# Six of eight depth chunks of each expert's gate and up product as three fp32r products, the rest parts of two of them by GpSimd

## The reference

```python
def expert_block(args):
    xb, gb = args
    h = jax.nn.silu(jnp.einsum('td,edf->tef', xb, w_gate)) * jnp.einsum('td,edf->tef', xb, w_up)
    return jnp.einsum('tef,efd->td', h * gb[:, :, None], w_down)
```

## Time and profile before

| | |
|---|---|
| times of three runs | 1206.55, 1212.63, 1216.0 us |
| the profiled execution: span from its first to its last instruction | 1206.0 us (the page gives no other time of it) |
| TensorE busy, matmuls | 1135.6 us, 94% |
| VectorE | 931.7 us, 77% |
| ScalarE | 482.0 us, 40% |
| GpSimd | 228.7 us, 19% |
| chain of waits | TensorE 88%, VectorE 5%, DMA 4%, ScalarE 2% |
| in the chain, by line | L758 18%, L785 15%, L763 14% |
| moved by DMA | 335.68 MB |

### The profile page before, as it was taken

One profiled execution on the slowest core, in us unless ns is written; L12 is line 12 of the kernel. 1 busy time (PEld: TensorE's weight loads), 2 busy tenths in 40 slices (PEclk: granted clock), 3 DMA queues, 4 the chain that ended last, 5 costly groups with the idle time before them and its releaser, 6 DMA issues.

```text
span 1206.0 us, 14783 instructions
## 1 busy us (share of the span) xinstructions
PE 1135.6 (94%) x4802; PEld 761.9 (63%) x4802; DVE 931.7 (77%) x1381; ACT 482.0 (40%) x622; POOL 228.7 (19%) x119
## 2 busy tenths in 40 slices
PE   2799999987999999999999999999999999999986
PEld 2453446875654477677777777777777777777632
DVE  4578997976533777998888888888888888888856
ACT  0214323345650022344444444444444444444411
POOL 0000000000000000122222222222222222223660
PEclk9799999998999989999999999999999999999998
DMA  9993421209202063799999999999999999999892
GB/s 349 369 397 85 50 27 70 71 19 347 89 16 90 35 267 117 299 366 388 382 385 380 384 386 379 373 386 373 397 382 381 377 375 385 373 379 398 319 374 114
DMA packets 77817, 335.68 MB, mean 278 GB/s; under 512 B 14376, under 2 KB 16296, under 8 KB 52824
## 3 DMA queue, kind: packets, MB, share of 16 engines
q1 hardware_dynamic: 58680, 293.15, 64.6%
q0 software_dynamic: 13824, 33.58, 7.6%
q10 hardware_dynamic: 5280, 8.53, 2.1%
HBM read 309.51 MB, written 42.48 MB: 292 GB/s over the span
## 4 chain that ended last, share of the span: by engine, by line
PE 88%; DVE 5%; DMA 4%; ACT 2%; issue 1%; ACTq 0%; SPq 0%; DVEq 0%; POOLq 0%
PE ps L758 18%; PE ps L785 15%; PE ps L763 14%; PE ps L1528 8%; PE ps L813 5%; PE ps L1758 5%; PE ps L1536 3%; PE ps L823 2%; PE ps L1599 2%; DMA ring<-in_w_ada 2%; PE ps L1622 2%; PE ps L1612 2%; PE ps L1728 2%; PE ps L880 1%; PE ps L1556 1%; PE ps L771 1%
## 5 line engine op out<-in xcount | busy, mean ns | idle before, releaser
L567 POOL DMA_INDIRECT xg<-u_rows,idx x64 | 182.7, 2855 | 489.2 <-DVE idx L1056 488.9
L758 PE MATMUL ps<-wx,xT 128*128 128x512 f32 x512 | 235.4, 602 | 0.0
L927 DVE TENSOR_TENSOR gu_lo<-wx,gu_hi 128x2048 fp32r<-128x2048 f32 x64 | 146.6, 2291 | 57.0 <-ACT gu_hi L646 57.0
L922 DVE TENSOR_TENSOR wd_lo<-wx,wd_hi 128x2048 fp32r<-128x2048 f32 x65 | 148.5, 2285 | 2.8 <-ACT wd_hi L1486 2.2
L758 PEld LDWEIGHTS ps<-wx,xT 128*128 128x128 f32 x512 | 92.1, 190 | 91.9 <-issue 91.8
L659 ACT ACTIVATE hs<-ps 128x256 f32<-128x256 f32 x68 | 26.1, 383 | 302.3 <-PE ps L763 281.7
L639 ACT ACTIVATE wd_hi<-wx 128x2048 fp32r<-128x2048 f32 x64 | 122.5, 1913 | 26.6 <-PE ps L785 26.6
L763 PE MATMUL ps<-gu_hi,xT_hi 128*128 128x512 f32 x256 | 126.2, 493 | 0.4 <-DVE gu_lo L927 0.4
L646 ACT ACTIVATE gu_hi<-wx 128x2048 fp32r<-128x2048 f32 x64 | 122.1, 1908 | 0.0
L785 PE MATMUL ps<-wd_hi,hT_hi 128*128 128x512 f32 x272 | 111.8, 411 | 2.9 <-DVE hT_lo L941 2.9
L785 PE MATMUL ps<-wd_hi,hT_lo 128*128 128x512 f32 x272 | 107.3, 395 | 0.0
(11 more groups left out here) (317 smaller groups left out, 1873.8 us busy)
## 6 DMA issues: line engine op xcount, KB each, us to landing
wx<-in_w_gate SPq DMA_DIRECT2D x64, 1024.0 KB, 7.8
wx<-in_w_up SPq DMA_DIRECT2D x64, 1024.0 KB, 10.9
wx<-in_w_down SPq DMA_DIRECT2D x64, 1024.0 KB, 8.5
expert_rows<-yrow SPq DMA_DIRECT2D x64, 512.0 KB
ring<-in_w_ada SPq DMA_DIRECT2D x7, 2048.0 KB, 19.1
ring<-in_w_in SPq DMA_DIRECT2D x6, 2048.0 KB, 15.9
vg<-in_w_ada SPq DMA_DIRECT2D x2, 2048.0 KB, 13.1
fk<-in_w_ada SPq DMA_DIRECT2D x2, 2048.0 KB, 14.9
```

The source lines that it names most:

```text
L567: pool.indirect_dma_start(out=xg[:, buf, :], out_offset=None, in_=u2_d[:, :], in_offset=bass.IndirectOffsetOnAxis(ap=idx[:, col:col + 1], ...
L758: pe.matmul(bank, xT_raw[:, j - J3, :], raw[:, :, j, :], start=(j == J3), stop=False)
L922: dve.tensor_tensor(wd_lo[s][:], w, wd_hi[:].bitcast(F32), ALU.subtract).then_inc(wd_ready, 1)
L927: dve.tensor_tensor(gu_lo[s][:, :, 0:J3, :], gate_up_weights(s)[:, :, 0:J3, :], gu_hi[:].bitcast(F32), ALU.subtract).then_inc(gu_lo_ready, 1)
```

## The change

J3, the number of split chunks, goes from 4 to 6; JA = 4 is the first group. TensorE multiplies two chunks in full, then the twelve products of chunks 0 to 3, then six products of chunks 4 and 5. The weights' high parts of chunks 4 and 5 get a buffer and a ScalarE instruction of their own (gu_hi2, gate_up_high2); their rest parts are made by GpSimd (gate_up_low2) into the same gu_lo. A new semaphore, gu_half, tells when the first twelve products are done; gate_up_high waits for that and stands ahead of silu. The turned rows' parts are made in two pieces, chunks 4 and 5 (from ps3) first. hT_hi moves into space shared with another tile.

```diff
-J3 = 4
+JA, J3 = 4, 6
...
+            def gate_up_low2(s, n):
+                pool.wait_ge(gu_hi2_ready, n + 1)
+                pool.tensor_tensor(gu_lo[s][:, :, JA:J3, :], gate_up_weights(s)[:, :, JA:J3, :], gu_hi2[:].bitcast(F32),
+                                   ALU.subtract).then_inc(gu_lo2_ready, 1)
...
-            def expert(i, u):
+            def expert(i, u, ending=False):
 
-                pool.wait_ge(idx_ready, i + (u + 3))
-                pool.reg_add(last, zero, T - 1)
-                gather((u + 2) % 4, u % 2, last)
+                if not ending or u < UNROLL - 2:
+                    pool.wait_ge(idx_ready, i + (u + 3))
+                    pool.reg_add(last, zero, T - 1)
+                    gather((u + 2) % 4, u % 2, last)
+                if not ending or u < UNROLL - 1:
+                    gate_up_low2((u + 1) % UNROLL, i + (u + 1))
...
             pairs(0, 7)
-            expert(tail, 1)
+            expert(tail, 1, True)
             pool.wait_ge(gu_done, n_steps + (VIRT - 2))
             pairs(1, 7)
             pool.wait_ge(y_stored, 16 * n_steps)
             pairs(0, 5)
             pairs(1, 5)
+            expert(tail, 2, True)
...
                 if used is not None:
+                    act.wait_ge(gu_half, used - VIRT)
+                act.activation(gu_hi[:], gate_up_weights(s)[:, :, 0:JA, :], ACT.Copy).then_inc(gu_hi_ready, 1)
+
+            def gate_up_high2(s, used):
+                if used is not None:
                     act.wait_ge(gu_done, used)
-                act.activation(gu_hi[:], gate_up_weights(s)[:, :, 0:J3, :], ACT.Copy).then_inc(gu_hi_ready, 1)
+                act.activation(gu_hi2[:], gate_up_weights(s)[:, :, JA:J3, :], ACT.Copy).then_inc(gu_hi2_ready, 1)
 
             def rows_high(n):
                 act.wait_ge(xt2_done, n + 1)
-                act.activation(xT_hi[:], ps[2][:, 0:J3 * P].rearrange("p (j n) -> p j n", n=P), ACT.Copy).then_inc(xt2_act, 1)
+                act.activation(xT_hi[:, JA:J3, :], ps[3][:, 0:(J3 - JA) * P].rearrange("p (j n) -> p j n", n=P),
+                               ACT.Copy).then_inc(xt2_act, 1)
+                act.activation(xT_hi[:, 0:JA, :], ps[2][:].rearrange("p (j n) -> p j n", n=P), ACT.Copy).then_inc(xt2_act, 1)
...
+                if more:
+                    gate_up_high((u + 1) % UNROLL, 8 * i + (32 if u < UNROLL - 1 else 64), i + (VIRT + u + 1))
                 silu_gate(i + (VIRT + u), u)
                 if more:
                     rows_high(i + (u + 1))
                     if first and u == 0:
                         shared_out(3)
-                    gate_up_high((u + 1) % UNROLL, 8 * i + (32 if u < UNROLL - 1 else 64), i + (VIRT + u + 1))
+                    gate_up_high2((u + 1) % UNROLL, i + (VIRT + u + 1))
...
-                pe.wait_ge(xt2_dve, n - VIRT + 1)
+                pe.wait_ge(xt2_dve, 2 * n - 2 * VIRT + 2)
                 pe.wait_ge(gu_lo_ready, n - VIRT + 1)
-                for j in range(J3):
-                    for k, (a, w) in enumerate(((xT_hi, gu_hi), (xT_hi, gu_lo[u]), (xT_lo, gu_hi))):
-                        mm = pe.matmul(bank, a[:, j, :], w[:, :, j, :], start=False, stop=(j == J3 - 1 and k == 2))
+                for j in range(JA):
+                    for a, w in ((xT_hi, gu_hi), (xT_hi, gu_lo[u]), (xT_lo, gu_hi)):
+                        mm = pe.matmul(bank, a[:, j, :], w[:, :, j, :], start=False, stop=False)
+                mm.then_inc(gu_half, 1)
+                pe.wait_ge(gu_lo2_ready, n - VIRT + 1)
+                for j in range(JA, J3):
+                    rest = gu_lo[u][:, :, j, :]
+                    for k, (a, w) in enumerate(((xT_hi, gu_hi2[:, :, j - JA, :]), (xT_hi, rest), (xT_lo, gu_hi2[:, :, j - JA, :]))):
+                        mm = pe.matmul(bank, a[:, j, :], w, start=False, stop=(j == J3 - 1 and k == 2))
                 mm.then_inc(gu_done, 1)
...
             def rows_low(n):
-                dve.wait_ge(xt2_done, n + 1)
-                dve.tensor_copy(xT_raw, ps[3][:, 0:(KD - J3) * P].rearrange("p (j n) -> p j n", n=P)).then_inc(xt_raw_ready, 1)
+                dve.wait_ge(xt2_act, 2 * n + 1)
+                dve.tensor_copy(xT_raw, ps[3][:, (J3 - JA) * P:].rearrange("p (j n) -> p j n", n=P)).then_inc(xt_raw_ready, 1)
                 dve.wait_ge(xt_raw_ready, n + 1)
-                dve.wait_ge(xt2_act, n + 1)
-                dve.tensor_tensor(xT_lo[:], ps[2][:, 0:J3 * P].rearrange("p (j n) -> p j n", n=P), xT_hi[:].bitcast(F32),
-                                  ALU.subtract).then_inc(xt2_dve, 1)
+                dve.tensor_tensor(xT_lo[:, JA:J3, :], ps[3][:, 0:(J3 - JA) * P].rearrange("p (j n) -> p j n", n=P),
+                                  xT_hi[:, JA:J3, :].bitcast(F32), ALU.subtract).then_inc(xt2_dve, 1)
+                dve.wait_ge(xt2_act, 2 * n + 2)
+                dve.tensor_tensor(xT_lo[:, 0:JA, :], ps[2][:].rearrange("p (j n) -> p j n", n=P),
+                                  xT_hi[:, 0:JA, :].bitcast(F32), ALU.subtract).then_inc(xt2_dve, 1)
```

More of the change, by code:

```diff
@@ L107, in build @@
             hT_lo = sb("hT_lo", [P, 2, KF, P], F32R, at=over)
+            hT_hi = sb("hT_hi", [P, 2, KF, P], F32R, at=over)
         vg = sb("vg", [P, NT, 2, 512])
         with ExitStack() as over:
-            gu_hi = sb("gu_hi", [P, 2, J3, ED], F32R, at=over)
+            gu_hi = sb("gu_hi", [P, 2, JA, ED], F32R, at=over)
         with ExitStack() as over:
@@ L202, in build @@
         hs = sb("hs", [P, 2, ED])
-        hT_hi = sb("hT_hi", [P, 2, KF, P], F32R)
         sel1 = sb("sel1", [P, 2, NT, P], BF16)
@@ L409, in build @@
         gu_lo_ready = sem("gu_lo_ready")
+        gu_hi2_ready = sem("gu_hi2_ready")
+        gu_lo2_ready = sem("gu_lo2_ready")
+        gu_half = sem("gu_half")
         y_stored = sem("y_stored")
@@ L420, in build @@
         out_stored = sem("out_stored")
+        gu_hi2 = sb("gu_hi2", [P, 2, J3 - JA, ED], F32R)
         tri8 = sb("tri8", [P, 64])
@@ L574, in pool_tail @@
                 gather(k, k)
+            gate_up_low2(0, 0)
             n_steps = steps(pool)
@@ L591, in pool_tail @@
             tail = pool.snap(pool.to_reg(n_steps - UNROLL), min_val=NE - UNROLL, max_val=MAXPASS * NE)
-            expert(tail, 0)
+            expert(tail, 0, True)
             def rows_of(t, k):
@@ L682, in act_tail @@
             gate_up_high(0, 32, None)
+            gate_up_high2(0, None)
             silu_gate(2, 2)
@@ L882, in gated @@
                 mm.then_inc(yg_summed, 1)
-            pe.wait_ge(xt2_act, n_steps)
-            pe.wait_ge(xt2_dve, n_steps)
+            pe.wait_ge(xt2_act, 2 * n_steps)
+            pe.wait_ge(xt2_dve, 2 * n_steps)
             pe.wait_ge(idx_ready, n_steps)
```

2 lines of the change are left out of this document (1 added, 1 removed).

## The result

The changed kernel took 1221.16 us (median of 4 runs, 1214.94 to 1234.65) beside 1210.07 for the kernel before: a ratio of 1.007 (95% interval 1.0038 to 1.0103; it leaves the run at 1234.65 out as disturbed). It is slower by a little, where I forecast 1210 and no measurable change. The profiled runs have spans of 1213.0 and 1206.0 us, 7.0 apart.

The account below looks back on a forecast made before the run. TensorE alone was taken as the bound, 10.27 us per expert. 57 x 0.33 = 18.8 us saved, 16 lost: -2.8 us, hence 1210 us, no measurable change; its own range 1200 to 1222, with rivals 1193 to 1335.

Parts of the forecast that it names:

- TensorE's saving: Per expert, 4 full records less and 6 split products more: 0.33 us less, a period of 9.94 us.
- Who goes first in the loop: Both subtracts ready near T+2.9, T being the next rows' first turn; VectorE's gu_lo first by 0.02 to 0.06 us.
- the other side: Rival: GpSimd's subtract goes first in every expert, TensorE starts 1.86 us late each time, 1315 us; chance 0.27.
- GpSimd's subtract: Rest parts of chunks 4 and 5: 2.2 us of work, row about 4.5 us with its wait for gu_lo.
- The step that failed: Experts with a 1.21 us VectorE instruction before gu_lo: GpSimd gets in first, 2.7 us net lost, five times, 13.6 us.
- forecast -2.8: Whole span: 18.8 us saved in 57 experts less 16 us lost elsewhere, on a span of 1206.0 us.
- The expert of rows 9: First expert, which already waits for gu_lo in the kernel before: gets some 2 us later.
- The tail: Behind the loop, two GpSimd subtracts stand between row fetches: 0 to 2 us.
- so gu_lo goes first and the loss is 0.4: Last expert of the tail: GpSimd still issues fetches until 1133.8, so VectorE's gu_lo precedes its subtract; loss 0.4 us.
- Rival 4 (the memory): Loop's weight loads fall 0.23 us behind per expert; some 4 us lost, with no room 1223 us; chance 0.07.

Follow-up runs that it names:

- experiment 2: Changed kernel with GpSimd's subtract replaced by a plain write of zeros, rest parts of chunks four and five left out: 1196.89 us, ratio 0.9883.
- experiment 4: Changed kernel with three extra TensorE products filling the stall in five experts: 1226.88 us, ratio 1.012; an earlier version with six products took 1232.26.
- experiment 5: Changed kernel with two row fetches at the end moved ahead of GpSimd's subtract of the last expert but one: 1231.86 us, inconclusive as a time.
- experiment 9: The changed kernel run again with no edit: 1214.97, 1216.84, 1230.91 and 1233.55 us, ratio 1.0146.
- e18: Changed kernel with each row fetch of the loop bringing half a row, the other half left out: 1215.46 us, ratio 1.0046.
- e1: Changed kernel with one added wait, GpSimd's subtract starting only when VectorE's gu_lo is done: 1207.23 us, ratio 0.9972.
- e7: Changed kernel; GpSimd's subtract waits for gu_lo, two end fetches go before the subtract, one_hots stands behind hT_lo: 1205.35 us, ratio 0.9942.
- e9: e7 without its moved end fetches, and with VectorE making the rest parts of the last three experts: 1198.73 us, ratio 0.9904.
- e10: e9 with the shared expert's operations moved out of the first and last experts to behind the loop: 1188.54 us, ratio 0.9835.

## Why the prediction was wrong

- **TensorE's saving: right.** 9.93 us against a forecast of 9.94, in 55 periods.
- **Who goes first in the loop, and for how long: right.** I had the margin at 0.02 to 0.06 us in VectorE's favour; it is 0.09. That is less than what I could tell beforehand (0.34 against 0.27 for the other side), so being right here is in part luck. GpSimd's subtract, which no row of the kernel before showed, was taken as 2.2 us between 0.95 and 4.5; it is 2.22 to 2.40 without the wait, and its row 4.45, as forecast. That the two exclude each other was read from the fetches; gu_lo's rows (2.28 and 4.45) show it for long instructions. The Trainium skill's SBUF — State Buffer, "Who interferes with whom", has it so (a VectorE instruction with two SBUF inputs against a GpSimd one that reads SBUF); the traces agree, also that a write is free (experiment 2: gu_lo 2.29 us beside it). The Trainium skill's GPSIMD Engine Reference, section 3.1, gave an estimated 2.3 us for the subtract; the trace agrees (2.22 to 2.40).
- **The step that failed:** "so TensorE starts 8.83 - 5.78 = 3.05 us late, 2.7 net. I count five of these, 13.6 us." The place, the cause and the cost of the standing hold (2.60 us). The term is mis-sized: it counts the standing and not what TensorE's clock does afterwards, some 1.5 us behind four of the six stalls, the second expert's among them (experiment 4 takes it away). That is 6 of the 9.8 us between the forecast -2.8 and the 7.0 of the spans; most of the rest is in the next two terms. I put the clock at nothing without a reason. In the experts the trace of before has only a stall of 0.45 us, with 0.31 us to the next product; but at its end TensorE stands for 2.32 us, and the granted clock behind that is 0.50 (timeline, and table by stretches):

```profile
1152.56 13.95 PE L880 MATMUL ps<-wx,xT 128*128 128x512 f32 x28 [2.32 <-DMA wx<-expert_rows,slot8i]
```

```profile
1152.70:1156.00 3.30, 3.30 (x4) 1.25 (x5) 3.23 (x4) 0.00 (x0) 2.39 (x4) 0.50 0.88 240
```

- **The expert of rows 9** was to lose "some 2 us". GpSimd started 0.5 us ahead of L1123 there, held that too (2.91 us in place of 1.21), and the stall is 4.10 us against 0.45: 3.65 more, and the clock. Without GpSimd it would have been 2.40 (experiment 2): about 1.7 of the 3.65 are GpSimd's. The rest I put down to the two full chunks less ahead of the wait (1.71 us of TensorE's work); no run tests that alone.
- **The tail:** "0 to 2 us" for two subtracts between row fetches; 4.0. I had counted GpSimd's busy time and not the 4.3 us in which the subtract stands at the head of the queue with fetches behind it (experiment 5 moves them ahead), nor that the last subtract would hold wd_lo. And "so gu_lo goes first and the loss is 0.4" in the last expert is a race that went either way in two traces of the kernel. Only both parts of the end together are steady: 11.7 and 10.9 us (experiment 9), where I had 5.8 and 0 to 2.
- **Rival 4 (the memory)** was given 0.07 and a loss of 4 to 13 us. In the two profiled executions it does not happen. In others the times speak for it: 1230.91 and 1233.55 beside 1214.97 in experiment 9, without a trace of one. Where no execution tips (e18, with half rows) the kernel is still slower by 0.5%, so the mis-sized terms alone turn the forecast gain into a loss.

Open: what makes the loop tip, and why kernels in which GpSimd's subtract waits for gu_lo did not in 33 executions (e1, e7, e9, e10), though they move the same at the same pace; and why of two equal stalls one lowers the clock and one does not.

## What to carry to other kernels

Work given to GpSimd beside a VectorE that reads two SBUF tiles is not parallel work: count it as time that VectorE loses, and look at what stands just ahead of VectorE's critical instruction, since a waiting GpSimd gets in behind that. Price a TensorE stall like those here (2 to 4 us) with the 1.5 us of slow products that mostly came behind it, and an in-order queue by the wait at its head. Take two traces of one kernel before you explain where in it the time went. When a loop with a DMA share of 0.99 is made shorter, look at several executions before believing one trace.
